# Second half's scale columns made on TensorE from the weights, full modulated rows made on VectorE

## What is computed

```python
c_act = jax.nn.silu(c)
mod = (c_act @ ada_w[l] + ada_b[l])[:, None, :]
sh1, sc1, g1, sh2, sc2, g2 = jnp.split(mod, 6, axis=-1)
u = _rmsnorm(h, norm1_g[l]) * (1 + sc1) + sh1
```

## Time and profile before

| | us |
|---|---|
| median of 3 runs | 1233.4 |
| lowest and highest | 1233.11, 1236.43 |
| profiled execution, device time | 1233.88 |
| its span, first to last instruction | 1232.1 |

### The profile page before, as it was taken

The page is one execution under the profiler, slowest core; times in us unless marked ns, Lnnn a source line. Parts: engine busy times, 40 slices in busy tenths (PEclk is TensorE's granted clock), DMA queues, the critical chain, the costliest instruction groups (busy, mean ns, idle before and its releaser), DMA issues.

```text
span 1232.1 us, 20837 instructions
## 1 busy us (share of the span) xinstructions
PE 1192.7 (97%) x5729; PEld 703.4 (57%) x5730; DVE 690.8 (56%) x1281; ACT 541.3 (44%) x630; POOL 222.4 (18%) x323
## 2 busy tenths in 40 slices
PE   5899999999999999998999999999999999999996
PEld 5687887777888888884444343443434434344342
DVE  4542347586572676867545454454545546555567
ACT  5572224745422413231435454454544546566521
POOL 1000000000000000003332332333323234343300
PEclk9799999999999999999999999999999999999999
DMA  9633503353495485655798889888888888999796
GB/s 342 209 107 115 187 5 103 103 200 126 153 343 186 141 276 197 222 198 240 291 354 326 319 321 340 309 335 314 308 339 301 329 307 326 382 403 417 279 417 268
DMA packets 88593, 321.56 MB, mean 261 GB/s; under 512 B 13040, under 2 KB 16344, under 8 KB 66152
## 3 DMA queue, kind: packets, MB, share of 16 engines
q1 hardware_dynamic: 69192, 279.69, 61.5%
q0 software_dynamic: 14432, 32.85, 7.0%
q10 hardware_dynamic: 4928, 8.49, 2.0%
HBM read 292.35 MB, written 48.24 MB: 276 GB/s over the span
## 4 chain that ended last, share of the span: by engine, by line
PE 90%; DVE 4%; DMA 3%; ACT 2%; SPq 1%; issue 1%; DVEq 0%; ACTq 0%
PE psum L1713 33%; PE psum L1947 28%; PE psum L1957 14%; PE psum L1936 4%; DMA w_now<-expert_rows 2%; PE psum L1686 2%; PE psum L1815 1%; PE psum L1986 1%; PE psum L1746 1%; DMA ring<-in_ada_w 1%; PE psum L1775 1%; PE psum L1804 1%; PE psum L1871 1%; PE psum L1727 1%; PE psum L1863 1%
## 5 line engine op out<-in xcount | busy, mean ns | idle before, releaser
L1947 PE MATMUL psum<-w_now,xT 128*64 128x512 f32 x1568 | 347.3, 595 | 0.0
L1947 PEld LDWEIGHTS psum<-w_now,xT 128*64 128x64 f32 x1568 | 108.2, 137 | 197.2 <-issue 195.9
L1957 PE MATMUL psum<-w_now,mask 128*64 128x512 f32 x784 | 176.6, 592 | 0.0
L1020 ACT ACTIVATE w_now<-stage 128x2048 f32 x79 | 147.7, 1906 | 37.2 <-issue 33.6
L482 DVE TENSOR_TENSOR w_lo<-ring,w_hi 128x1024 fp32r<-128x1024 f32 x80 | 94.7, 1222 | 86.0 <-ACT w_hi L475 84.0
L747 POOL COPY w_now<-stage 128x1024 f32 x79 | 82.0, 1055 | 335.5 <-PE psum L1957 314.6
L1713 PE MATMUL psum<-uT_hi,w_hi 128*128 128x512 f32 x352 | 139.3, 396 | 1.1 <-DVE w_lo L482 1.1
L1713 PE MATMUL psum<-uT_hi,w_lo 128*128 128x512 f32 x352 | 137.0, 389 | 0.0
L1713 PE MATMUL psum<-uT_lo,w_hi 128*128 128x512 f32 x352 | 136.9, 389 | 0.0
L475 ACT ACTIVATE w_hi<-ring 128x1024 fp32r<-128x1024 f32 x80 | 82.7, 1056 | 122.1 <-PE psum L1713 59.5
L1531 DVE COPY w_now<-stage 128x2048 f32 x79 | 95.5, 1242 | 45.7 <-issue 42.0
(11 more groups left out here) (361 smaller groups left out, 1666.4 us busy)
## 6 DMA issues: line engine op xcount, KB each, us to landing
stage<-in_exp_w_gu SPq DMA_DIRECT2D x106, 1024.0 KB, 8.4
stage<-in_exp_w_down SPq DMA_DIRECT2D x53, 1024.0 KB, 5.9
ring<-in_w_in SPq DMA_DIRECT2D x56, 512.0 KB, 5.5
expert_rows<-zero_fill SPq DMA_DIRECT2D x16, 1024.0 KB, 8.2
ring<-in_ada_w SPq DMA_DIRECT2D x32, 512.0 KB, 5.0
stage<-expert_rows SPq DMA_DIRECT2D x12, 1024.0 KB, 18.8
ring<-in_ada_w SPq DMA_DIRECT2D x4, 1024.0 KB, 13.4
scale_w<-in_ada_w SPq DMA_DIRECT2D x4, 1024.0 KB, 14.7
```

The lines of the kernel that those rows point to most:

```text
L1020: act.activation(w_now[:, q, 2:4], staged(turns[q] + STAGES - 1, 2, 2), ACT.Copy).then_inc(gu_moved[1], 1)
L1947: mm = pe.matmul(moe_bank(GU)[at, :], xT[:, s % 2, k, at], gu_part(q, k), start=(k == 0), stop=(k == KT - 1))
L1957: mm = pe.matmul(moe_bank(Y0 + g)[at, :], hT[:, j, at], dn_part(q, j, g), start=(j == 0), stop=(j == 1))
```

## The change

The second half's scale columns are no longer summed on VectorE. TensorE makes them straight from `scale_w[:, 1]`, in one job of a zero product and 8 x 4 one-column products, placed after the columns of the first half. `ACT_FULL`, the semaphore `u_full` and ScalarE's full values are gone; VectorE makes all eight full values with `u_whole`, 0 to 3 after `scale_cols(0)` and 4 to 7 after `scale_cols(1)`. `scale_cols(1)` now stands after the low parts 0 and 1, and the low part of the rank weights after the full values 4 to 7. GpSimd waits for `row_sum` of 2 and for the new job.

```diff
@@ gpsimd
-            pool.wait_ge(row_sum, 3)
+            pool.wait_ge(row_sum, 2)
+            wait_job(pool, ("scale", 1))
             pool.memset(wlr_lo.bitcast(F32), 0.0).then_inc(lr_zero, 1)
@@ scalar, u_parts(k)
-                if k in ACT_FULL:
-                    act.activation(full_of(k), xnT[:, k], ACT.Identity, bias=mod_cols[:, k:k + 1], scale=mod_cols[:, KT + k:KT + k + 1]).then_inc(u_full, 1)
@@ vector
             def u_lo(k):
-                if k in ACT_FULL:
-                    dve.wait_ge(u_full, k + 1)
                 dve.wait_ge(u_hi, k + 1)
...
-            sum_rows(scale_w[:, 1], scale_in[1], tmpT[:, 1], range(4))
...
             scale_cols(0)
-            sum_rows(scale_w[:, 1], scale_in[1], tmpT[:, 1], range(4, KT))
-            for k in range(4):
+
+            def u_whole(ks):
+
+                for k in ks:
+                    wait_emptied(dve, ("xT", k))
+                    own(ts(full_of(k), xnT[:, k], mod_cols[:, KT + k:KT + k + 1], mod_cols[:, k:k + 1], ALU.mult, ALU.add))
+                own.settle()
+
+            u_whole(range(4))
+            for k in range(2):
                 u_lo(k)
+            scale_cols(1)
+            for k in range(2, 4):
+                u_lo(k)
+            u_whole(range(4, KT))
             dve.wait_ge(lr_split, 1)
             dve.wait_ge(lr_zero, 1)
             tt(wlr_lo[:, :, :, 0:RANK], wlr_four, wlr_hi[:, :, :, 0:RANK].bitcast(F32), ALU.subtract).then_inc(lr_split, 1)
-            scale_cols(1)
-            for k in (6, 7):
-                wait_emptied(dve, ("xT", k))
-                own(ts(full_of(k), xnT[:, k], mod_cols[:, KT + k:KT + k + 1], mod_cols[:, k:k + 1], ALU.mult, ALU.add))
-            own.settle()
             for k in range(4, KT):
                 u_lo(k)
@@ tensor
             columns(("scale", 0), 2, tmpT[:, 0])
-            columns(("scale", 1), 3, tmpT[:, 1])
+            start_job(("scale", 1))
+            pe.matmul(bank(("scale", 1))[:, 0:4], ident[:], zeros[:, 0:4], start=True, stop=False)
+            for k in range(KT):
+                pe.wait_ge(scale_in[1][k // 4], 16)
+                for j in range(4):
+                    mm = pe.matmul(bank(("scale", 1))[:, j:j + 1], scale_w[:, 1, k, j * P:(j + 1) * P], c_col[:, k:k + 1], start=False, stop=(k == KT - 1 and j == 3))
+            end_job(mm)
```

More of the change, by code:

```diff
@@ L326, in layer_program @@
         row_sum = sem("row_sum")
-        u_full = sem("u_full")
         xn_ready = sem("xn_ready")
@@ L451, in raw @@
             return ring[:, 0, PK * p:PK * p + PK]
-        ACT_FULL = (0, 1, 2, 3, 4, 5)
         def full_of(k):
```

## The result

The changed kernel took 1246.93 us in the median of its three runs (1243.86 to 1249.76), against 1233.4 (1233.11 to 1236.43). The ratio is 1.0099, with a 95% interval from 1.0066 to 1.0132: slower, as forecast, and 2.7 us above the forecast of 1244.2, inside its range. The profiled execution took 1249.76, span 1248.0, mean granted clock 0.983. It is the slowest of the three, so its 15.9 us over the span of before are more than the typical cost.

What follows compares the result with a forecast made beforehand. TensorE was taken to bound the kernel, which slides as a block from low-rank product "lr" on. "lr" starting at 51.54 instead of 40.73 adds 10.8 us to 1233.88; less 0.5 for the median, 1244.2 us, range 1242 to 1247.

Steps and rivals of the forecast that it cites:

- What bounds, and that the kernel slides as a whole: Whole kernel: TensorE, busy 97%, bounds it; everything from low-rank product "lr" on shifts together, with one later wait of 1.1 us.
- The stream's pace, 0.218 and not 0.116: TensorE's second scale columns: 64 one-column instructions at 0.218 us each, the lower clock level, 14.4 us in all, done at 47.0.
- rival B: One-column stream at the upper clock level: columns done at 40.24, "lr" 4.05 us later, about 1237.4 us; chance 0.07.
- rival C: Clock rises somewhere inside the one-column stream; rising halfway gives +7.4 us, 1240.8 us; chance 0.06.
- Rival D: Not slower: the clock stays up through the stream and idle time into "lr", +1.6 us, 1235.0 us; chance 0.04.
- The order on VectorE, 4.54 us: VectorE after the second columns: work queued behind that wait, rank weights' low part last, delays "lr" 4.54 us, to 51.54.
- The start of the stream, 32.58: TensorE's one-column stream starts at 32.58 us, where the two column products end, less a 0.15 us overlap.
- "lr" itself, 7.94 us, half a microsecond either way: Low-rank product on TensorE: starts at the lower clock level in both kernels, same 7.94 us, give or take half a microsecond.
- GpSimd's wait moved, free: GpSimd's two memsets after the new product: end at 48.0 and 48.9, costing nothing unless 3 us later.
- Free ScalarE, 4.3 us: ScalarE in the setup: its six full rows go, 4.3 us of its time; its last high row is not late.
- The base: Starting time of the sum: the profiled execution of the kernel before, 1233.88 us, with the median of runs 0.5 below.
- sum of 10.8: Total added time: "lr" starts at 51.54 instead of 40.73, so the kernel takes 10.8 us longer.

Runs made afterwards that it cites:

- e7_burst: The changed kernel with added work, 20 bf16 products of 512 columns in one piece ahead of the one-column stream: 1252.99 us (one run).
- e4_wide: The changed kernel with added work, 16 bf16 products of 512 columns mixed into the one-column stream, two per k: 1249.97 us (one run).
- e1_order: The changed kernel with low parts 2 and 3 and the rank weights' low part moved ahead of the second columns on VectorE: 1241.94 us, ratio 1.0056.
- e9_after: The changed kernel unaltered, timed again with more runs against the kernel before: 1246.33 us (6 runs), ratio 1.0082.
- e2_stream: The kernel before with only TensorE's one-column stream in place of VectorE's second sum, ScalarE's full rows kept: 1242.39 us, ratio 1.0049.
- e3_rows: The kernel before with only the full rows changed, all eight made by VectorE, four ahead of the low parts: 1238.12 us, ratio 1.0013.

## Why the prediction was right, point by point

- *What bounds, and that the kernel slides as a whole.* Right in kind: no wait of TensorE behind "lr" shrank, and the one of 1.1 us is there after with 1.1. The sentence that nothing after "lr" runs to a clock of its own was wrong in the plain sense. The granted clock dips again at the two-column matmuls and can dip at the final sums. How long a dip lasts changes from execution to execution, and in the profiled one the two added 3.3 us. Two readings of the prediction were a little off without weight in the sum: the first V product comes 7.94 us after the start of "lr" (48.67 - 40.73) and not 8.11, which is how long its 24 matmuls take to their end, and the slices of 0.57 and 0.61 put the clock's fall at 32.1 and its rise at 45.8, not at 32.4 and 45.6.
- *The stream's pace, 0.218 and not 0.116.* Right: 13.79 us for 64, and e7_burst shows that the clock sets it. The two rows that I leaned on, the pace of the first L1746 group and the fall during work, were the right ones. The Trainium skill's advice to keep TensorE busy without gaps (page "TensorE: Matmul & The Clock Gate", section "Why this matters for your kernels"), weighed in the prediction, would have put the end of the stream at 40.2. The stream has no gap and the clock stayed down, so rival B fell with it, and so did rival C (no rise in 14 us, nor in 19 with e4_wide). Rival D fell too: "lr" started at 0.50.
- *The order on VectorE, 4.54 us.* Right: 4.40 measured, and 4.2 gained at the V product when e1_order takes it away.
- *The start of the stream, 32.58.* This is the term that was mis-sized for the profiled execution. The stream began at 35.3, for the clock fell near 30.4 instead of 32.1, and rose later in the transposes (6.57 us instead of 5.71). The groups ahead of the stream, which both kernels have, took 0.72 and 1.40 us more. I had allowed for an earlier or later fall only inside the stream and not ahead of it. In e9_after, e1_order and e2_stream, where the fall was at 31.5 to 32.1, the stream starts at 32.4 to 32.5, as forecast.
- *"lr" itself, 7.94 us, half a microsecond either way.* 7.87 in e9_after and 8.25 in e1_order, within that; 7.32 in the profiled execution, 0.1 us outside it, since the clock rose 3.8 us after its start, and in before some 5 us after it (45.8 - 40.73).
- *GpSimd's wait moved, free.* Right here: the first memset ran from 49.65 and was done before it was wanted. But I said that a memset costs only if it is late. e3_rows shows the cost that I did not have, a memset beside full rows on VectorE. In the changed kernel the second memset and the full rows hardly meet (the memset ends at 51.5, and four rows from 51.17 take 1.97 us).
- *Free ScalarE, 4.3 us.* Right that it bought nothing (e2_stream against e1_order).
- *The base.* I summed on a profiled execution at 1233.88 whose clock was the best of four steps. The kernel before costs 1236 to 1237 in the median of more runs, and the change 9.4 us by the medians of e9_after and 10.1 by its ratio (7.5 to 12.6), close to the sum of 10.8; the first three runs of each made it 13.5. That 1246.9 lies in the forecast's 1242 to 1247 is therefore in part luck: it is at the edge, and the base of the first three runs was 2.5 to 3.6 us lower than that of more runs (1233.4 against 1235.9 and 1236.96). What the traces bear out is the added time and its two parts.

What stays open: why the clock falls at 30.4 in one execution and at 32.1 in another of the changed kernel, and why it dips at the final sums in one and not in the other. It was seen and not tried.

## What to carry to other kernels

A long run of one-column products keeps TensorE's row full and still runs at half the clock: short groups behind the transposes had the upper level (32 instructions in 3.71 us), but the stream of 64 took 13.79 us, did not win the level back, and "lr" behind it started at 0.50. Price such a run at the lower level, and ask what dense work comes right after it. When an instruction stream gains a wait for a late result, put everything that does not need the result ahead of the wait, above all what the next engine is waiting for. Before adding up microseconds on one profile, look at the mean clock of all runs: a difference of 0.005 went with 6 us here and no edit had caused it.

## What was not expected of the hardware

- A full row on VectorE (one tensor input, 128x512 fp32) took 0.48 us each alone (four in 1.91), and 1.38 and 1.25 us beside GpSimd memsets of 128x1024 (e3_rows); sums and subtractions with two tensor inputs kept 0.75 and 0.68 us beside them.
- 16 wide bf16 products among 64 one-column instructions, 1.01 us of every 2.37, left the clock at 0.50 for 19 us; 20 of them in a row brought it to 1.00 in 3.9 us, and it was lost again 4.5 us into one-column products.
- In 24 runs of one kernel the mean granted clock took four values (0.991, 0.989, 0.988, 0.986), and its time followed them in steps over 6.3 us; in 17 other runs 0.987 came too. The final sums alone took 5.4 us in some profiles and 7.1 in others, of the changed kernel both.
